# Making the first expert product of one block in four ahead of the experts, in 4-byte matmuls, through DRAM

## What is computed

```python
q = (hb @ w_pq).reshape(t, 8, 2, 128)
s = einsum('thpk,hpnk->thpn', q, peer_keys)      # two scores of 128 keys per head
sv, si = top_k(s, 16)                            # 16 + 16 best, 256 sums, 16 best of these
e, g = (expert numbers, softmax of the sums)     # 8 heads x 16 picks per token
a = gelu(einsum('thkd,td->thk', peer_u[e], hb))
y = einsum('thk,thkd->td', g * a, peer_v[e])
```

## Time and profile before

| | |
|---|---|
| median of 3 runs | 4070.72 us (4058.43 to 4075.23) |
| the profiled execution's own time | 4065.13 us |
| its span (first to last instruction) | 4063.3 us |
| PE, PEld busy | 3284.5 us (81%), 2772.6 us (68%) |
| DVE, ACT, POOL busy | 3008.0 us (74%), 1042.9 us (26%), 1648.1 us (41%) |
| mean granted clock of TensorE | 0.864 |

### The profile page before, as it was taken

The page is one execution under the profiler, slowest core; times in us unless marked ns, Lnnn a source line. Parts: engine busy times, 40 slices in busy tenths (PEclk is TensorE's granted clock), DMA queues, the critical chain, the costliest instruction groups (busy, mean ns, idle before and its releaser), DMA issues. The chain is left out here.

```text
span 4063.3 us, 57177 instructions
## 1 busy us (share of the span) xinstructions
PE 3284.5 (81%) x19892; PEld 2772.6 (68%) x19892; DVE 3008.0 (74%) x5897; ACT 1042.9 (26%) x1915; POOL 1648.1 (41%) x1320
## 2 busy tenths in 40 slices
PE   7665548787689889675663776999999999999997
PEld 4435424455455555334663666999999999999997
DVE  3316968678576777374998996888888888888886
ACT  2211112223122222111110553222232222222321
POOL 0004535346555655264455773333323333333232
PEclk9577779667787888777776888999999999999998
DMA  3032158468798887586100236888878888788786
GB/s 116 8 129 86 31 206 286 155 215 276 268 319 276 294 291 245 206 321 234 32 26 1 117 149 247 276 275 277 282 270 278 286 278 274 274 276 279 276 277 219
DMA packets 303822, 876.75 MB, mean 216 GB/s; under 512 B 34009, under 2 KB 125450, under 8 KB 292554
## 3 DMA queue, kind: packets, MB, share of 16 engines
q0 software_dynamic: 147456, 536.94, 39.0%
q1 hardware_dynamic: 154170, 334.15, 22.7%
q10 hardware_dynamic: 2016, 3.67, 0.2%
HBM read 819.17 MB, written 55.74 MB: 215 GB/s over the span
## 5 line engine op out<-in xcount | busy, mean ns | idle before, releaser
L109 POOL DMA_INDIRECT x_got<-v,x_expert x512 | 562.4, 1098 | 1062.9 <-DVE x_y L130 541.1
L109 POOL DMA_INDIRECT x_got<-u_rows,x_expert x512 | 613.8, 1199 | 659.8 <-DVE x_y L130 294.7
L130 DVE SCALAR_TENSOR_TENSOR x_y<-x_got,x_hidden,x_y 128x1024 f32<-128x1024 f32 x512 | 656.1, 1281 | 40.5 <-DMA x_got<-v,x_expert 38.0
L123 DVE SCALAR_TENSOR_TENSOR x_got<-x_got,x_y 128x1024 f32<-128x1024 f32 x512 | 626.7, 1237 | 43.8 <-DMA x_got<-u_rows,x_expert 42.2
L1667 PE MATMUL e_a<-h2h,e_uh 128*128 128x272 f32 x2048 | 590.4, 288 | 19.4 <-DVE e_ul L1745 19.4
L1669 PE MATMUL e_a<-h2h,e_ul 128*128 128x272 f32 x2048 | 594.0, 290 | 0.0
L1684 PE MATMUL e_y<-e_wh,e_vh 128*128 128x272 f32 x2048 | 588.9, 288 | 3.0 <-DVE e_wl L1768 3.0
L1668 PE MATMUL e_a<-h2l,e_uh 128*128 128x272 f32 x2048 | 589.2, 288 | 0.0
L1685 PE MATMUL e_y<-e_wl,e_vh 128*128 128x272 f32 x2048 | 588.7, 287 | 0.0
L1686 PE MATMUL e_y<-e_wh,e_vl 128*128 128x272 f32 x2048 | 587.7, 287 | 0.0
L1667 PEld LDWEIGHTS e_a<-h2h,e_uh 128*128 128x128 f32 x2048 | 386.3, 189 | 19.6 <-issue 19.6
(11 more groups left out here) (376 smaller groups left out, 5805.4 us busy)
## 6 DMA issues: line engine op xcount, KB each, us to landing
e_u<-uT SPq DMA_DIRECT2D x128, 512.0 KB
e_v<-v SPq DMA_DIRECT2D x64, 1024.0 KB
gates_d<-g_stage SPq DMA_DIRECT2D x8, 4352.0 KB
e_gate<-gates_d SPq DMA_DIRECT2D x32, 1088.0 KB
d_page<-page SPq DMA_DIRECT2D x128, 144.0 KB
d_latent<-page_rows SPq DMA_DIRECT2D x128, 128.0 KB
t0r_w<-w_pq SPq DMA_DIRECT2D x16, 512.0 KB
x_got<-u_rows,x_expert POOLq DMA_INDIRECT x512, 5.8
```

The costliest lines, as they stand in the source:

```text
L109: pool.indirect_dma_start(out=self.got[n % RING_G][:], out_offset=None, in_=self.tables[phase], in_offset=bass.IndirectOffsetOnAxis(ap=sel ...
L123: dve.scalar_tensor_tensor(out=row[:], in0=row[:], scalar=1.0, in1=self.y[g][:], op0=ALU.mult, op1=ALU.mult, accum_out=self.hidden[:, g, k ...
L130: dve.scalar_tensor_tensor(out=self.y[g][:], in0=row[:], scalar=self.hidden[:, g, k:k + 1], in1=self.y[g][:], op0=ALU.mult, op1=ALU.add).t ...
```

## The change

A new class `Ahead` makes a = gelu(u_j x h) for each block j = 4n + 3 (32 of the 128 blocks), with unsplit 4-byte operands, one matmul where `make_a` has three. 24 of them are made in the late router, three per head, and 8 in `gate_matrix`, one matmul or none after each group of four tokens. Two new SBUF buffers hold u, two the result; ACT evicts each half with Gelu; SP stores each block (272 KB) to the DRAM tensor `ahead_d`. `mixer_out` writes an unsplit copy of h for the five dense tiles. The router's loop over heads is written out, its transposes have two buffers instead of three (the PSUM banks are needed), and SP loads the weights of a head after it has stored and loaded for the head before. In `experts` PE makes three blocks instead of four before each set of values; SP loads the made block; the ring of u has three buffers instead of four.

```diff
+class Ahead:
+    COUNT = NK // 4
...
+    def load(self, sp, count=1):
+        for n in range(self.loaded, min(self.loaded + count, self.COUNT)):
+            after(sp, s["h_a"], NB * (n - 1))
+            sp.dma_start(self.u[n % 2][:], self.table[4 * n + 3]).then_inc(s[f"h_uin{n % 2}"], 16)
...
+    def store(self, sp, count=1):
+            sp.wait_ge(s["h_gelu"], NB * n + NB)
+            sp.dma_start(self.spill[n], self.out[n % 2][:]).then_inc(s[f"h_st{n % 2}"], 16)
...
+    def product(self, pe, count):
+            n, (b, k) = step // (NB * KD), divmod(step % (NB * KD), KD)
+            if k == 0:
+                pe.wait_ge(s[f"h_uin{n % 2}"], 16 * (n // 2) + 16)
+                after(pe, s["h_gelu"], NB * (n - 1) + b + 1)
+            mm = pe.matmul(self.bank[b][:, 0:TD], self.u[n % 2][:, k, :], self.h2[:, k, b * TD:(b + 1) * TD],
+                           start=k == 0, stop=k == KD - 1)
...
+    def evict(self, act, count=1):
+            act.wait_ge(s["h_a"], half + 1)
+            act.activation(self.out[n % 2][:, b * TD:(b + 1) * TD], self.bank[b][:, 0:TD],
+                           ACT.Gelu).then_inc(s["h_gelu"], 1)
@@ mixer_out, ACT
+                if t0 + t >= TG:
+                    act.activation(full[:, :, (t0 + t - TG) * P:(t0 + t - TG) * P + n], h2T[:, :, 0:n],
+                                   ACT.Copy).then_inc(s["o_hf"], 1)
@@ router, heads, SP and PE
-            with eng.Fori(0, H // 2 - 1) as i:
-                first(2 * i + 1, 1, tail(2 * i, 0), False)
-                first(2 * i + 2, 0, tail(2 * i + 1, 1), False)
-            first(H - 1, 1, tail(H - 2, 0), True)
+            for m in range(1, H):
+                first(m, m % 2, tail(m - 1, (m - 1) % 2), m == H - 1)
...
+            for m in range(H):
                 for e in range(2):
                     j = 2 * m + e + 2
+                    if j < HP:
+                        sp.wait_ge(s["r_wl"], 2 * m + e + 1)
+                        weights(j, e)
+                for n in range(blocks_ahead):
+                    ahead.store(sp)
+                    ahead.load(sp)
...
                 for b in range(QB):
                     queries(2 * m, 0, b)
+                ahead_part(0)
                 queries(2 * m + 1, 1, 0)
                 score(2 * m, 0)
+                ahead_part(1)
                 for b in range(1, QB):
                     queries(2 * m + 1, 1, b)
                 score(2 * m + 1, 1)
+                ahead_part(2)
@@ gate_matrix, PE
                 mm.then_inc(s["g_mm"], 1)
+                ahead.product(pe, pieces(q))
@@ experts, PE, ACT and DVE
-                for c in range(1, 5):
-                    make_a(8 * i + c, c % 2)
+                for n in (1, 2, 3):
+                    make_a(6 * i + n, n % 2)
                 add_values(2 * i, (0, 1, 2, 3))
-                for c in range(5, 8 if last else 9):
-                    make_a(8 * i + c, c % 2)
+                for n in (4, 5) if last else (4, 5, 6):
+                    make_a(6 * i + n, n % 2)
                 add_values(2 * i + 1, (4, 1, 2, 3))
...
-                    if not last or c < 7:
-                        split_u(8 * i + c + 1, (c + 1) % 2)
+                    if c % 4 < 3 and (not last or c < 6):
+                        split_u(6 * i + c // 4 * 3 + c % 4 + 1)
...
-                    dve.wait_ge(s["e_gelu"], NB * j + b + 1)
+                    if j % 4 < 3:
+                        dve.wait_ge(s["e_gelu"], NB * (j // 4 * 3 + j % 4) + b + 1)
+                    else:
+                        dve.wait_ge(a_in[j // 4 % 2], 16 * (j // 8) + 16)
```

More of the change, by code:

```diff
@@ L973, in _, with mixer_out @@
             dve.memset(oT, 0.0).then_inc(s["d_zero"], 1)
-def mixer_out(nc, a, t0, t1, part, gather, steps, gelus):
+def mixer_out(nc, a, t0, t1, part, full, gather, steps, gelus):
     with ExitStack() as ctx:
@@ L1183, in _, with router @@
             tiles(dve, pool, rest)
-def router(nc, a, t0, t1, queries_of, picks, gather, g0, g1):
+def router(nc, a, t0, t1, queries_of, picks, gather, g0, g1, ahead, blocks_ahead):
     with ExitStack() as ctx:
@@ L1303, in _ @@
                     pe.wait_ge(s["c_pk"], 2 * PICK * H)
[L1304 removed]
+                after(pe, s["c_ev"], n - 1)
                 for k in range(3):
[L1306 removed]
+                    mm = pe.transpose(turn[n % 2][:, k * P:(k + 1) * P], out[:, k, t, :], ident[:])
                 mm.then_inc(s["c_tr"], 1)
@@ L1497, in gate_matrix, with pieces, halves @@
         stored = [s["g_st0"], s["g_st1"]]
+        todo = NB * KD * ahead.COUNT - ahead.made
+        def pieces(q):
+            return (q + 1) * todo // GROUPS - q * todo // GROUPS
+        def halves(q):
+            return (q + 1) * todo // GROUPS // KD - q * todo // GROUPS // KD
         block = ctx.enter_context(nc.Block())
@@ L1502, in _ @@
             sp.dma_start(iota[:], a["iota"]).then_inc(s["g_in"], 16)
+            done = NB * KD * ahead.COUNT - todo
             for b in range(GB):
+                while ahead.stored * NB * KD < done + (b + 1) * todo // GB - NB * KD:
+                    ahead.store(sp)
+                    ahead.load(sp)
                 sp.wait_ge(s["g_ev"], (b + 1) * NG)
@@ L1506, in _ @@
                              stage[b % 2][:].rearrange("p i t -> p (i t)")).then_inc(stored[b % 2], 16)
+            ahead.store(sp, ahead.COUNT)
+            ahead.settle(sp)
             for e in range(2):
@@ L1554, in _ @@
                     continue
+                ahead.evict(act, halves(q - LAG))
                 b, g = divmod(q - LAG, NG)
@@ L1582, in experts @@
         gate = [sb(f"e_gate{r}", [P, GB, 4, GT]) for r in range(2)]
+        made = [sb(f"e_made{r}", [P, DT]) for r in range(2)]
         wf = [sb(f"e_wf{b}", [P, TD]) for b in range(NB)]
@@ L1595, in experts, with weights @@
         GBB = GB // NB
+        def weights(j, b):
+            return wf[b][:] if j % 4 < 3 else made[j // 4 % 2][:, b * TD:(b + 1) * TD]
         def freed(m, n):
@@ L1636, in body @@
                 for c in range(1, 9):
-                    if not last or c < 5:
-                        load_u(8 * i + c + 3, (c + 3) % U_RING)
+                    ahead = c // 4 * 3 + c % 4 + 2
+                    if c % 4 < 3 and (not last or ahead < 6):
+                        load_u(6 * i + ahead, 8 * i + ahead // 3 * 4 + ahead % 3, ahead % U_RING)
+                    if c == 1:
+                        load_made(2 * i + 1, 1)
+                    if c == 5 and not last:
+                        load_made(2 * i + 2, 0)
                     if c == 1:
@@ L1922, in part @@
                     return dense[k][:, :, (t - TG) * P:min((t - TG + 1) * P, DT)]
-                mixer_out(nc, a, TA, TILES, part, gather, (6, 8), (1,))
-                with nc.sbuf_tensor("picks", [P, 3, NPAD - GTOK], F32) as picks:
+                mixer_out(nc, a, TA, TILES, part, full, gather, (6, 8), (1,))
+                with ExitStack() as picking:
+                    picks = sb(picking, "picks", [P, 3, NPAD - GTOK])
+                    ahead = Ahead(nc, picking, a, full)
                     late = GTOK - TA * P
                     blocks = [(0, late, (h2h, h2l), 0)] + [(late + b * TD, TD, dense, b * TD) for b in range(NB)]
-                    router(nc, a, TA, TILES, blocks, picks, gather, TA, TG)
-                    gate_matrix(nc, a, picks)
+                    router(nc, a, TA, TILES, blocks, picks, gather, TA, TG, ahead, 3)
+                    gate_matrix(nc, a, picks, ahead)
             begun = gather.planned + RING_G
```

127 lines of the change are left out of this document (88 added, 39 removed).

## The result

| | before | after |
|---|---|---|
| median | 4069.98 us (12 runs) | 4083.51 us (12 runs, 4073.32 to 4090.24) |
| ratio after / before | | 1.0037, 95% interval 1.0023 to 1.0051 |
| span of the profiled execution | 4063.3 us | 4085.9 us |
| mean granted clock of TensorE | 0.864 | 0.874 |

A forecast was written before the change was run, and what follows sets the result against it. DVE was taken to bound the late router and gate matrix, PE the experts. Router +60, experts -26, gate matrix +2.5, settling +1 and the rest +0.5 gave +38 us on 4068: 4106 us, range 4055 to 4145.

The forecast's parts named there:

- PE becomes the router's bound, +60: Late router: three added blocks, 22.2 us a head, exceed PE's room of 15.8; heads go from 36.56 to 43.0 us, +60 us.
- The gate matrix, +2.5, and settling, +1: Gate matrix: added matmuls fit except in early groups at half clock, +2.5 us; settling the last store beside the gates', +1.
- The experts' chain: Experts: values wait for DVE's low part of the fourth weight, starting 21.3 us after the quad's start; PE waits 3.2 us.
- The experts' loss in clock, 31 x 2.0 = 62 us: Experts: PE's clock falls after the waits before the values, losing 2.0 us a quad, 62 us in all.
- both examples: Kernel before: waits of 2.98 us (last quad) and 3.36 us (mixer's end), followed by half clock, 3.05 and 1.9 us lost.
- The experts' gain before the clock, 31 x 2.85 = 88 us: Experts: each quad shortens from 24.15 to 21.3 us up to its values, 88 us over 31 quads.
- The rule that each round starts at the low clock: Experts: a loop whose matmuls wait each round starts each at low clock; 31 x 3.05 = 95 us lost.
- longer waits: Slower rival, experts: v late, full 3.05 us clock loss, or a second wait behind DVE; 4152 us, chance 0.14.
- the clock holds: Faster rival, experts: waits of 3 us pass without a fall of the clock; -24 us, 4044, chance 0.12.
- DVE stays the router's bound: No-change rival, late router: three blocks cost under 15.8 us or PE overtakes by its lead; -7 us, 4061, chance 0.10.
- The written-out loop, costed at nothing: Early router: writing out the loop costs nothing, a few us either way, since DVE hides the other engines' branches.
- The base: Whole kernel before the change: time taken as 4068 us, halfway between the profiled execution and the median of runs shown.

## Why the prediction was right or wrong

- **PE becomes the router's bound, +60: right.** 42.8 us between heads against 43.0 forecast, +58 in all; two blocks a head give 36.4. The room of 15.8 us and the 7.4 us of a block both held.
- **The gate matrix, +2.5, and settling, +1: right** at 8 blocks (+2.7 for both). With 16 PE takes over there too.
- **The experts' chain: right.** The values start 21.3 us after the quad's start, behind the link that was named, and the last quad gains next to nothing, as forecast.
- **The experts' loss in clock, 31 x 2.0 = 62 us: this term failed.** Measured are 34 us in time, 1.1 a wait, or 41 by the granted clock, 1.3 a wait; filling the wait puts it at 38. The step that erred was "since both examples show a fall, but not each wait need hit the same, I take 2.0": both examples were waits with a fall after them, so they said nothing of how often there is none. 11 of the 31 waits have none, and where the clock falls the common loss is 1.7 us, below both examples (1.9 and 3.05).
- **The experts' gain before the clock, 31 x 2.85 = 88 us: 10 too high.** It was reckoned up to the start of the values only. From there to the next quad it is 24.15 us even where the clock doesn't fall, against 23.84 before, so a quad gets 2.5 us shorter and 31 of them 78. What makes this 0.3 us a quad no run shows. The two errors pull against each other: 78 - 34 = 44 us, where 88 - 62 = 26 were forecast. Had the gain been sized right, the forecast would have been 48 us instead of 38, still further off.
- **The rule that each round starts at the low clock**, from the page "TensorE: Matmul & The Clock Gate", section "HAM oscillation — how this bites in real kernels", of the Trainium skill, was weighed at 95 us. The runs show a fall after two waits in three only, so it would have put the time further off; and its case, *longer waits* (4152), didn't come.
- **The rivals.** That the clock holds would have given the experts -88 us, and that DVE stays the router's bound 45 us less there: neither came, though 4061 was as near the result as 4106, by a mechanism that isn't there.
- **The written-out loop, costed at nothing: right by luck.** The early router's queries take 170 to 173 us in the kernels where the other engines' loops are written out, against 175 before and 176 with TensorE's alone: a small gain. But the same edit alone costs 75 us in a later stage, and in the changed kernel, whose loop in the experts is shorter, it happened not to. "A few us either way" was no bound: nothing in the trace of before showed how near the experts' loop was to its limit.
- **The base**: forecast 4068, measured 4070. The stage sum of +18 against the +13.5 of the medians is within what the unchanged stages differ between executions (the start of the late router moved by up to 32 us). Of the 24.5 us between forecast and result, 18 are in the experts.

## What to carry to other kernels

Work moved to "where PE is idle" pays up to the room of that stage and costs in full from there: measure the room per turn and fill it, no further (two blocks a head were -20 us, three +14). When an engine's work is cut below its supplier's chain, the chain's order is the next thing to change, together with the queue that feeds it (on top of two blocks a head that took the ratio from 0.9952 to 0.9771, 74 us). After any edit that changes the length of TensorE's program ahead of a long loop, compare the packets of the instruction queue over that loop; if they have risen, a padding of cheap instructions may be worth more than the edit.

## What the runs showed of the hardware

- TensorE's instruction fetch: a loop with 1536 matmuls and weight loads in a round ran free (2 packets of the instruction queue in 1250 us) or was fetched anew each round (109 packets), by the length of TensorE's program ahead of it; that cost 83 us on a stage of 1543.
- The clock after a wait of 2.8 to 3.9 us, repeated 31 times: no fall after 11 of them, 1.7 us lost after 16, 3.4 after 4. Useless matmuls in the wait kept it at 1.00 and were worth 33 us of the stage.
- 4-byte matmuls of 272 columns: two records each, 0.229 us apart from start to start at full clock in each of the 24 blocks of the late router (0.231 was taken). The record's own mean of 393 ns holds time of flight.
- 200 waits that are already met cost TensorE's sequencer about 10 us: from the last query product to the gate matrix it is 76.4 us with them, 66.1 in the kernel with all loops written out and 66.7 in that with the early loops alone, 0.05 us each.
